# Experts: the residual added behind the seventh group's scatter, its inputs unscaled on VectorE, and six constant products ahead of the last downs

## The reference

```python
def hierarchical_moe(h, w_rg, b_rg, w_re, b_re, w_gate, w_up, w_down):
    ...
    w_top = jax.nn.softmax(top_v, axis=-1) * g_w
    expert_id = g_sel[:, None] * EXPERTS_PER_GROUP + top_i
    combine = jnp.sum(jax.nn.one_hot(expert_id, N_EXPERTS, dtype=jnp.float32) * w_top[..., None], axis=1).astype(t.dtype)
    hg = jnp.einsum('td,edf->tef', t, w_gate)
    hu = jnp.einsum('td,edf->tef', t, w_up)
    act = jax.nn.silu(hg) * hu * combine[:, :, None]
    y = jnp.einsum('tef,efd->td', act, w_down)

        h = h + hierarchical_moe(rms_norm(h, norm_moe[i]), w_router_group[i], b_router_group[i],
                                 w_router_expert[i], b_router_expert[i], w_exp_gate[i], w_exp_up[i], w_exp_down[i])
```

## Time and profile before

| | |
|---|---|
| median of three runs | 1045.06 us (1042.41 to 1046.19) |
| profiled execution | 1045.58 us |
| its span, first to last instruction | 1043.8 us |
| mean granted clock of TensorE | 0.984 of 2.4 GHz |
| busy: PE, DVE, ACT | 95%, 60%, 50% of the span |
| moved by DMA | 241.74 MB |

### The profile page before, as it was taken

The page is one execution under the profiler, slowest core; times in us unless marked ns, Lnnn a source line. Parts: engine busy times, 40 slices in busy tenths (PEclk is TensorE's granted clock), DMA queues, the critical chain, the costliest instruction groups (busy, mean ns, idle before and its releaser), DMA issues.

```text
span 1043.8 us, 19513 instructions
## 1 busy us (share of the span) xinstructions
PE 990.7 (95%) x8590; PEld 914.7 (88%) x8590; DVE 626.5 (60%) x836; ACT 522.8 (50%) x741; POOL 19.7 (2%) x23
## 2 busy tenths in 40 slices
PE   7999999999999999999998787699999999999998
PEld 6999999899989999997665454399999999999998
DVE  6798789868676874444111110089984765555566
ACT  5576588844675573533211111178557555434453
POOL 0000021001000000000000000000000000000000
PEclk9999999999999999999999888899999999999999
DMA  7665453446235457789999999954421366455531
GB/s 290 243 240 180 187 192 132 159 165 237 86 130 215 143 222 270 313 358 390 399 420 420 421 421 420 413 201 162 155 89 38 135 243 241 167 198 202 198 126 41
DMA packets 34871, 241.74 MB, mean 232 GB/s; under 512 B 4064, under 2 KB 4448, under 8 KB 6368
## 3 DMA queue, kind: packets, MB, share of 16 engines
q1 hardware_dynamic: 33264, 233.32, 58.5%
q0 software_dynamic: 1232, 6.99, 1.9%
q10 hardware_dynamic: 288, 0.15, 0.1%
HBM read 239.36 MB, written 1.08 MB: 230 GB/s over the span
## 4 chain that ended last, share of the span: by engine, by line
PE 78%; DMA 9%; DVE 8%; ACT 3%; issue 1%; SPq 1%; DVEq 0%; ACTq 0%
PE ps L481 19%; PE ps L491 18%; PE ps L492 18%; PE ps L1284 4%; DMA raw<-in_c_weights 3%; PE ps L565 3%; DMA xlo<-in_c_weights 3%; DMA wr<-in_c_weights 3%; PE ps L1234 2%; DVE wlo L2057 2%; PE ps L1311 1%; PE ps L960 1%; PE ps L1322 1%; DVE xs L2289 1%; SPq L3067 1%
## 5 line engine op out<-in xcount | busy, mean ns | idle before, releaser
L2057 DVE TENSOR_TENSOR wlo<-raw,whi 128x2048 fp32r<-128x2048 f32 (+1 forms) x119 | 271.0, 2281 | 112.7 <-ACT whi L1395 112.3
L481 PE MATMUL ps<-XUh,whi 128*128 128x256 f32 x987 | 277.8, 281 | 0.5 <-DVE wlo L2057 0.4
L491 PE MATMUL ps<-XUl,whi 128*128 128x256 f32 x992 | 275.1, 277 | 0.0
L492 PE MATMUL ps<-XUh,wlo 128*128 128x256 f32 x992 | 274.7, 277 | 0.0
L1395 ACT ACTIVATE whi<-raw 128x2048 fp32r<-128x2048 f32 (+1 forms) x119 | 225.0, 1894 | 45.3 <-PE ps L492 38.7
L481 PEld LDWEIGHTS ps<-XUh,whi 128*128 128x128 f32 x987 | 185.7, 188 | 2.6 <-issue 1.7
L491 PEld LDWEIGHTS ps<-XUl,whi 128*128 128x128 f32 x992 | 186.5, 188 | 0.8 <-issue 0.5
L492 PEld LDWEIGHTS ps<-XUh,wlo 128*128 128x128 f32 x992 | 186.4, 188 | 0.0
L2990 DVE SCALAR_TENSOR_TENSOR sphs<-sphs,wsl,ps 128x256 f32<-128x256 f32 x8 | 3.8, 481 | 82.3 <-ACT sphs L2022 64.4
L481 PE MATMUL ps<-ffnah,whi 128*128 128x256 f32 x176 | 48.6, 276 | 0.0
L491 PE MATMUL ps<-ffnal,whi 128*128 128x256 f32 x176 | 48.6, 276 | 0.0
(11 more groups left out here) (632 smaller groups left out, 2361.2 us busy)
## 6 DMA issues: line engine op xcount, KB each, us to landing
raw<-in_c_weights SPq DMA_DIRECT2D x137, 1024.0 KB, 4.9
wr<-in_c_weights SPq DMA_DIRECT2D x36, 1024.0 KB, 25.2
xhi<-in_c_weights SPq DMA_DIRECT2D x12, 1024.0 KB, 25.3
xlo<-in_c_weights SPq DMA_DIRECT2D x12, 1024.0 KB, 25.9
extra<-in_c_weights SPq DMA_DIRECT2D x8, 1024.0 KB, 16.8
acb<-sums POOLq DMA_DIRECT2D x4, 1024.0 KB, 4.9
T<-in_c_weights SPq DMA_DIRECT2D x4, 1024.0 KB, 18.5
T8b<-in_c_weights SPq DMA_DIRECT2D x4, 1024.0 KB, 19.6
```

The source lines that it names most:

```text
L481: pe.matmul(ps, h, x, start=start, stop=False, skip_group_check=loose)
L491: pe.matmul(ps, h(k), xl(k), start=False, stop=False, skip_group_check=loose)
L492: t = pe.matmul(ps, l(k), xh(k), start=False, stop=stop and k == kt - 1, skip_group_check=loose)
L2057: dve.tensor_tensor(l[:, 0:n], r, h[:, 0:n].bitcast(F32), ALU.subtract).then_inc(*did("w_lo", "split", i))
```

## The change

1. The matrix `back` and its two DVE products are gone; DVE still computes `rback` = 1/rmoe.
2. `residual` leaves its place ahead of gather(1). In its place in the sums, the first scatter now starts them. The wait for the banks yb goes to the scatter.
3. Behind the copy of Y of group 6, DVE multiplies the two halves of XT with rback, in place.
4. `residual` stands behind scatter(6), ahead of the gate products of group 7, waits for those, and multiplies the unscaled XT with the plain identity.
5. In pe_last, `constant_products` with n = 6 stands behind the wait for the second last down piece (e = 30) and ahead of the wait for the last one.
6. The dense way gets the same residual, unscaled by DVE ahead of it.

The diff:

```diff
--- before.py
+++ after.py
@@ -415,7 +415,6 @@
     Xg = sb("Xg", [128, 8, 128], F32, xu_at + 4 * KB)
     XM, XM2 = sb("XM", [128, 8, 256], F32, xu_at), sb("XM2", [128, 8, 256], F32, xu_at + 8 * KB)
     Pg, shs = sb("Pg", [128, 2, 128], F32, rs_at), sb("sphs", [128, 256], F32, rs_at + KB)
-    back = sb("back", [128, 2, 128], F32, rs_at + 2 * KB)
     aT, PT = sb("aT", [128, 2, 128], F32, rs_at + 2 * KB), sb("PT_", [128, 256], F32, cst_at + 512)
     iota128, sid = slots[:, 0:128], slots[:, 128:144]
     T8d = sb("T8d", [128, 8, 256], F32, xu_at)
@@ -1172,9 +1171,10 @@
         yb = [dbank.take("dy", j, among=(4 + j,)) for j in range(4)]
         for _, free in yb:
             w.wait_ge(*free)
-        residual(pe, w, yb)
         for b in range(4):
             w.wait_ge(*at_("emptied", "dx", b))
+        w.wait_ge(*at_("dense", "unscaled"))
+        residual(pe, yb, True)
 
         def up(n, e):
             i = expert[n, e]
@@ -1216,14 +1216,13 @@
                 down(e)
         w.wait_ge(*at_("dense", "xg"))
 
-    def residual(pe, w, yb):
-
-        w.wait_ge(*at_("route", "back"))
+    def residual(pe, yb, first):
+
         for d in range(8):
             for j in range(2):
                 o = 256 * (d % 2) + 128 * j
-                t = pe.matmul(yb[d // 2][0][:, o:o + 128], XT[:, j, 128 * d:128 * d + 128], back[:, j, :],
-                              start=d % 2 == j == 0, stop=False, skip_group_check=True)
+                t = pe.matmul(yb[d // 2][0][:, o:o + 128], XT[:, j, 128 * d:128 * d + 128], ident,
+                              start=first and d % 2 == j == 0, stop=False, skip_group_check=True)
         return t
 
     def gather_half(pe, w, ps, g, q):
@@ -1313,13 +1312,15 @@
                             t.then_inc(*did("w_used", "used", i))
 
         def scatter(g):
+            for _, free in yb:
+                w.wait_ge(*free)
             w.wait_ge(*at_("moe", "pt", g))
             w.wait_ge(*at_("emptied", "down", g, 0))
             w.wait_ge(*at_("emptied", "down", g, 1))
             for d in range(8):
                 ps = yb[d // 2][0][:, 256 * (d % 2):256 * (d % 2) + 256]
                 c = slice(128 * d, 128 * d + 128)
-                t = pe.matmul(ps, Y[:, c], PT[:, :], start=False, stop=False, skip_group_check=True)
+                t = pe.matmul(ps, Y[:, c], PT[:, :], start=g == 0 and d % 2 == 0, stop=False, skip_group_check=True)
             t.then_inc(*did("moe_pe", "scattered", g))
 
         def first_tables():
@@ -1331,15 +1332,15 @@
             if g == 0:
                 spread_positions()
                 yb = [sbank.take("sy", j, among=(4 + j,)) for j in range(4)]
-                for _, free in yb:
-                    w.wait_ge(*free)
-                residual(pe, w, yb)
             gather(g + 1)
             if g:
                 scatter(g - 1)
             turn(g)
             down(g)
         scatter(6)
+        w.wait_ge(*at_("moe", "unscaled", 0))
+        w.wait_ge(*at_("moe", "unscaled", 1))
+        residual(pe, yb, False)
         up(7)
 
     def pe_last(pe, w):
@@ -1363,6 +1364,8 @@
         w.wait_ge(*at_("emptied", "turn"))
         for e in range(28, 32):
             w.wait_ge(*at_("loaded", expert["down", e]))
+            if e == 30:
+                constant_products(pe, dps[0][:, 0:128], 6)
         for f in range(2):
             for k in range(2):
                 for e in range(4):
@@ -2636,9 +2639,7 @@
         dve.tensor_tensor(comb[:, :, 0:32], comb[:, :, 0:32], place2[:, :, 0, :], ALU.add).then_inc(*did("route_dve", "route", "comb"))
         dve.tensor_tensor(pgrp[:, :, :, :], comb[:, :, 32:34].unsqueeze(1).broadcast_to([128, 8, 2, 2]),
                           rk[:, 0, 32:40].unsqueeze(2).unsqueeze(3).broadcast_to([128, 8, 2, 2]), ALU.add).then_inc(*did("route_dve", "route", "free"))
-        r_(dve.reciprocal(rback, rmoe))
-        for j in range(2):
-            dve.tensor_scalar(back[:, j, :], ident, rback[:, j:j + 1], None, ALU.mult).then_inc(*did("route_dve", "route", "back"))
+        dve.reciprocal(rback, rmoe).then_inc(*did("route_dve", "route", "back"))
 
 
         w.wait_ge(*at_("route", "flag"))
@@ -2954,6 +2955,10 @@
             w.wait_ge(*at_("dense", "x", b))
             dve.tensor_tensor(T8d[:, 2 * b:2 * b + 2, :], halves(dbank.ps("dx", b)),
                               col["norm_moe"][:, 2 * b:2 * b + 2].unsqueeze(2).broadcast_to([128, 2, 256]), ALU.mult).then_inc(*dbank.emptied("dx", b))
+        w.wait_ge(*at_("route", "back"))
+        for j in range(2):
+            t = dve.tensor_scalar(XT[:, j, :], XT[:, j, :], rback[:, j:j + 1], None, ALU.mult)
+        t.then_inc(*did("dense_dve", "dense", "unscaled"))
         for e in range(32):
             x = dhs[e % 4][:, :, :]
             w.wait_ge(*at_("emptied", "dup", "gate", e))
@@ -3009,6 +3014,11 @@
             if g:
                 w.wait_ge(*at_("scattered", g - 1))
             dve.tensor_copy(Y[:, 512:1024], sbank.ps("down", g, 1)[:, :]).then_inc(*sbank.emptied("down", g, 1))
+            if g == 6:
+                w.wait_ge(*at_("route", "back"))
+                w.wait_ge(*at_("gx", 7, 1))
+                for j in range(2):
+                    dve.tensor_scalar(XT[:, j, :], XT[:, j, :], rback[:, j:j + 1], None, ALU.mult).then_inc(*did("moe_dve", "moe", "unscaled", j))
 
 
     def pool_program(pool):
```

## The result

The changed kernel is slower: median 1045.47 us (1044.41 to 1047.61, 22 runs) against 1043.87 us (1040.14 to 1046.19, 22 runs) for the kernel before, on the same chip. The ratio is 1.002, with a 95% interval of 1.0011 to 1.0029, so 1.1 to 3.0 us. The forecast was 2.2 us faster than before. 1045.47 us lies within its range only because the range was built on a median of three runs of before that was 1.2 us above the median of 22.

The account below looks back on a forecast made before the run. The weights' DMA stream was taken to pace the experts' stage, TensorE nearly everything behind 700 us. Stream -1.3, hidden residual and scaling 0, clock -0.9 sum to -2.2 us, from 1045.06 to 1042.9 us; range 1040.3 to 1045.6 us.

Parts of the forecast that it names:

- What hides the residual: Ahead of group 7's up products: a 4.94 us wait for weights covers the residual's 3.84 us, cost 0.
- The stream: Start of the experts: without the early residual, weights flow without a dip at 507 to 510 us, -1.3 us.
- The products: Ahead of the last downs: six products start at 669.9 us, take 1.44 us, at worst delay downs 0.4 us.
- the downs starting at the end of the products: Last downs: sign of a wrong forecast if they start then instead of when the last piece lands.
- The clock: Last ups and downs: less idle time and the products raise TensorE's clock, -0.9 us, bounds +0.4 and -1.7.
- the last ups would run at 1.00: Group 7's up products: at the high clock, about 1.7 us shorter, as idle time ahead shrinks to 1.1 us.
- the hole and its cause: DMA rate dip at 507 to 510 us: wr loads issued late, awaiting the first downs; 1.29 us of streaming lost.
- rival 2: Start of the experts: the hole at 507 to 510 us has another cause and stays; 1044.2 us, 7%.
- the early issue of the wr loads: SP's queue, start of the experts: four loads issued 4.3 to 6.0 us earlier, near 501 to 503 us.
- the 4.3 us: Start of the experts: TensorE's shift without the early residual, 3.84 us work plus 0.69 us wait less overlap.
- rival 3: Experts' stage: TensorE paces it, so the 4.3 us shift passes whole to the end; 1039.9 us, 5%.
- Rival 4: Group 7: low clock stretches residual, gate products and ups beyond the slack of 1.1 + 2.85 us; 1047.5 us, 4%.

Follow-up runs that it names:

- e3: The changed kernel with the residual behind the last group-6 scatter called twice; 1050.42 us, ratio 1.0076 to the kernel before.
- e4: The changed kernel with TensorE's unused dense way and its branch left out of the program; 1041.93 us, ratio 0.9991 to the kernel before.
- e2: The kernel before with only the six products of ones added ahead of the last downs; 1043.76 us, ratio 1.0004 to the kernel before.
- e1: The changed kernel without the six products of ones, residual still behind the group-6 scatter; 1043.63 us, ratio 1.0005 to the kernel before.
- e5: The kernel before with the residual moved between group 6's gate and up products, without products of ones; 1044.42 us, ratio 1.0009 to the kernel before.
- e6: Same as e5 with the six products of ones ahead of the last downs; 1041.97 us, ratio 0.9991 to the kernel before.
- e8: e7 with 16 products of ones added at the end of the dense way, never executed; 1042.75 us, ratio 0.9991 to the kernel before.
- e9: The changed kernel with 16 products of ones added at the end of the dense way, never executed; 1046.61 us, ratio 1.0025 to the kernel before.
- e7: The kernel before without the residual in the sparse way, group 0's scatter starting the sums; 1046.25 us, ratio 1.0024 to the kernel before.

## Why the prediction was wrong

**The step that failed** is "What hides the residual: those end at 658.2 us, and TensorE then stands still for 4.94 us until the last up pieces land at 663.11 us." I read the start of the ups, 663.11 us, as the landing, because the row names a DMA as releaser. The landing could have been worked out from what the trace held: that piece was issued at 635.5 us and landed 27.0 us later, at 662.5 us. The 0.6 us between the two should have made me ask what else was going on. In before, the jump and the wait for the piece ended within a microsecond of each other, and the row named the one that ended first: the restart is 1.72 us behind the instruction packet, as in after, where no weights were awaited. So the gap should have been as long without the wait. The residual was priced at 0 and cost 3.57 us (after, e3; hidden in e4).

**The stream** was right in kind and too small: -1.3 forecast, -2.07 us at the issue of H. All kernels with the residual out of the early place show it: H is issued 161.1 to 161.4 us after the first gather's start, against 163.7 in before and 163.5 us in e2, which keeps the residual there. The filled windows account for some 1.4 us; the other 0.7 us (0.9 by this measure) I haven't found. But of the 2.07 only 0.97 us reached the scatter of group 6.

**The products** were placed behind a wait for e = 30 "so they start when it lands". Since TensorE came later and the weights earlier, both last pieces were there (670.4 us at the latest) before aT was (673.05), and 1.60 us went onto the path (after against e1: 1.6 us in the medians). The prediction allowed +0.4 us for late products, not this; the downs starting at the end of the products was one of its signs of being wrong.

**The clock** was priced at -0.9 us. In after the downs did run at the high clock, but so they did in e1 without products, where only 0.46 us of idle time stood ahead of them. Where the wait is real, the pair e5 and e6 (6.46 against 3.64 us, 1.9 us in the ratios) speaks for the products, e2's median for no gain on average, e4's 4.59 us against a sure effect, and e8's 3.64 us against their being needed behind every wait (its wait was shorter, 1.73 us against 2.36 in e5). What the products are worth stays open. The prediction cited the Trainium skill (TensorE: Matmul & The Clock Gate, part 1) for the number of slow matmuls differing from run to run. No kernel here was traced twice, but executions do differ: the mean granted clock of before's 23 beside e4 lies between 0.978 and 0.989. That before's 5.34 us of downs was one draw fits this and isn't shown. The forecast that the last ups would run at 1.00 fell with the cover; the windows of after, around the gap:

```profile
645.00:658.00 13.00, 11.73 (x98) 8.37 (x102) 2.18 (x4) 0.81 (x2) 0.00 (x0) 1.00 1.01 420
658.00:661.00 3.00, 2.76 (x52) 1.42 (x44) 0.00 (x0) 0.09 (x1) 0.00 (x0) 1.00 1.02 426
665.50:671.50 6.00, 5.82 (x64) 3.01 (x64) 0.00 (x0) 0.00 (x0) 0.00 (x0) 0.63 1.02 421
```

The clock is full up to 663 us, two microseconds into the gap, and at half speed from there to 669.5 us.

**Right**: the hole and its cause (rival 2 fell), the early issue of the wr loads (501.17 us, forecast 501 to 503), the DVE products at 0.70 us each, hidden under the scatter (forecast 0.7), and that the 4.3 us don't pass whole (rival 3).

**Rival 4** named the right sign and place, the residual ahead of the ups, with the wrong mechanism: it wanted the low clock in three stretches to eat the slack. Two of them stayed at 1.00, up to 661 us; the slack of 4.94 us wasn't there. The sum as measured, for the start of the downs: -0.97 (stream, as it arrives) + 3.57 (residual) - 0.18 (gap) + 0.53 (ups) + 1.60 (products) - 2.38 (the wait for the last piece, 2.85 us, of which 0.47 is left for aT) = +2.17 us.

## What to carry to other kernels

An idle stretch can hide work only if it is a wait for something that comes at its own time: before putting work there, compute when that thing lands (issue plus time to landing) and set it beside the restart. The idle stretch at the jump here moved with the work ahead of it and covered nothing, whatever releaser the row named. Filler for the clock goes only where a wait remains after all the other edits; where the wait is gone, as here, the filler stands on the critical path. And where an edit moves code behind a branch, a control with instructions that are never run tells its placement from its work.

## What the hardware showed unexpectedly

TensorE was idle for 4.76 to 4.98 us at its jump over some 1600 written instructions (two records for most, had they run) that aren't executed (after 4.76, e1 4.85, e3, e8 and e9 4.83, e7 4.98), while the weights streamed at some 420 GB/s, and one instruction packet fell into each of these gaps; without the branch and these instructions it was 0.60 us. A second idle time, 3.59 us, stood 12 matmul records behind the jump in e7 and went away when 16 more instructions that are never executed were put ahead of it (e8). So an edit that took matmuls out cost 2.5 us (e7's ratio) by where it left the code behind it. Whether the jump gets cheaper with the dense way placed elsewhere, behind pe_last, wasn't tried.

The kernel before varies from 1040.14 to 1046.19 us between executions; the slow downs of its profile are 1.70 us longer than e2's.
